# Two PSUM banks for the down products' halves, and five steps of VectorE and ScalarE moved up in a hybrid layer with sixteen experts

## The reference

```python
def reference(x, ...):                     # 1024 tokens x 1024, float32, one layer
    h = rms_norm(x, attn_norm_g)
    proj = h @ w_in                        # 1024 x 2824
    y_a = gated_delta_rule(...)            # 4 heads, chunks of 64, conv, gated norm
    y_b = swa_sink_attention(...)          # 8 query heads, 2 kv heads, window 128
    x = x + concatenate([y_a, y_b]) @ w_out
    return x + hier_moe(rms_norm(x, ffn_norm_g), ...)

def hier_moe(h, ...):                      # best of 4 groups, then best 2 of its 4 experts
    for e in range(16):
        gu = tok @ w_gate_up[e]            # 1024 -> 2 x 256
        act = silu(gu[:, :256]) * gu[:, 256:]
        y = y + gates[:, e:e + 1] * (act @ w_down[e])   # 256 -> 1024
    return y
```

## Time and profile before

| what | value |
|---|---|
| median of 3 runs | 946.41 us (943.29 to 948.25) |
| the profiled execution | 948.48 us, of which the span is 946.6 us |
| mean granted TensorE clock of it | 0.986 |
| TensorE busy | 889.7 us (94%) |
| VectorE busy | 603.7 us (64%) |
| ScalarE busy | 330.1 us (35%) |
| GpSimd busy | 222.6 us (24%) |
| HBM traffic | 137.7 MB, 145 GB/s over the span |

### The profile page before, as it was taken

The page is one execution under the profiler, slowest core; times in us unless marked ns, Lnnn a source line. Parts: engine busy times, 40 slices in busy tenths (PEclk is TensorE's granted clock), DMA queues, the critical chain, the costliest instruction groups (busy, mean ns, idle before and its releaser), DMA issues.

```text
span 946.6 us, 16441 instructions
## 1 busy us (share of the span) xinstructions
PE 889.7 (94%) x6148; PEld 591.6 (62%) x6148; DVE 603.7 (64%) x1746; ACT 330.1 (35%) x877; POOL 222.6 (24%) x302
## 2 busy tenths in 40 slices
PE   5999899999999999999999999789889999899986
PEld 5787587696696777768769656465533453433432
DVE  2367776785785787587678577868445535466443
ACT  1343331431432432332143134123363633646610
POOL 7020020020010001002002000300345546565643
PEclk9999999999999999999999999999989999999998
DMA  8920101010010120110100003703557968889621
GB/s 308 396 113 1 45 24 45 9 61 23 24 67 1 46 68 1 46 46 23 46 22 3 23 24 130 292 24 120 182 193 262 365 212 271 329 288 347 204 69 59
DMA packets 51052, 113.87 MB, mean 120 GB/s; under 512 B 11783, under 2 KB 13063, under 8 KB 50960
## 3 DMA queue, kind: packets, MB, share of 16 engines
q1 hardware_dynamic: 34064, 87.07, 25.8%
q0 software_dynamic: 14592, 25.22, 7.5%
q10 hardware_dynamic: 2304, 0.33, 0.2%
HBM read 112.56 MB, written 25.17 MB: 145 GB/s over the span
## 4 chain that ended last, share of the span: by engine, by line
PE 83%; DVE 10%; ACT 2%; issue 2%; DMA 1%; another core or an unknown queue 1%; POOL 0%; ACTq 0%; DVEq 0%; POOLq 0%
PE pm L432 77%; PE pm L435 5%; DVE pqkv L1519 2%; PE pm L836 1%; ACT ctmp L1247 1%; ACT pT L1247 1%; DMA qkvT<-h_mid,w_sb 0%; DMA xt<-in_x 0%; DVE xT L1342 0%; ACT pqkv L1038 0%; DVE xT L1455 0%; DVE X L1701 0%; DVE bs L1763 0%; DVE sc L1687 0%
## 5 line engine op out<-in xcount | busy, mean ns | idle before, releaser
L432 PEld LDWEIGHTS pm<-hT,w_sb 128*128 128x128 f32 x1544 | 176.6, 194 | 5.8 <-DVE hT L1471 3.0
L432 PE MATMUL pm<-hT,w_sb 128*128 128x128 f32 x1544 | 177.7, 277 | 2.3 <-DVE hT L1471 2.3
L432 PE MATMUL pm<-w_sb,hT 128*128 128x512 f32 (+1 forms) x384 | 153.8, 543 | 0.0
L432 PE MATMUL pm<-wo_sb,pT 128*128 128x512 f32 x320 | 143.9, 597 | 2.7 <-ACT pT L1110 1.4
L2071 POOL TENSOR_TENSOR tail<-tail,rows 128x512 f32<-128x512 f32 x8 | 10.8, 1344 | 483.9 <-ACT aTm L1059 483.9
L432 PEld LDWEIGHTS pm<-w_sb,hT 128*128 128x128 f32 x384 | 70.1, 193 | 51.8 <-issue 46.2
L432 PEld LDWEIGHTS pm<-wo_sb,pT 128*128 128x128 f32 x320 | 58.4, 190 | 68.0 <-issue 63.8
L1519 DVE SCALAR_TENSOR_TENSOR pqkv<-ci,cw,pqkv 128x128 f32<-128x128 f32 x288 | 77.4, 344 | 13.9 <-ACT pqkv L1038 13.8
L432 PE MATMUL pm<-w_sb,ctmp 128*128 128x512 f32 (+1 forms) x200 | 74.2, 601 | 0.6 <-DVE ctmp L1853 0.6
L432 PE MATMUL pm<-w_sb,Y 128*128 128x512 f32 x96 | 49.7, 637 | 8.4 <-issue 3.4
L1247 ACT ACTIVATE pT<-aTm 32x256 f32<-32x256 f32 x128 | 53.0, 414 | 9.6 <-DVE aTm L1930 8.1
(11 more groups left out here) (346 smaller groups left out, 1500.1 us busy)
## 6 DMA issues: line engine op xcount, KB each, us to landing
w_sb<-in_w_gate_up SPq DMA_DIRECT2D x12, 2048.0 KB
w_sb<-in_w_down SPq DMA_DIRECT2D x12, 1024.0 KB
wo_sb<-in_w_gate_up SPq DMA_DIRECT2D x4, 2048.0 KB
w_sb<-in_w_in SPq DMA_DIRECT2D x3, 2048.0 KB, 21.1
xt<-in_x SPq DMA_DIRECT2D x8, 512.0 KB, 4.6
xT<-in_x_turned SPq DMA_DIRECT2D x8, 512.0 KB, 3.8
w_sb<-in_w_in SPq DMA_DIRECT2D x4, 1024.0 KB, 13.0
wo_sb<-in_w_out SPq DMA_DIRECT2D x1, 4096.0 KB, 22.0
```

The lines of the kernel that those rows point to most:

```text
L432: return pe.matmul(o_, lhsT=l_, rhs=r_, start=start, stop=stop, skip_group_check=True)
```

## The change

1. `down_bank`: the left half of a whole tile's down product goes to pm[4], the right half to pm[5] (for all experts but the last, which has pm[1] and pm[0] as before). The right half waits for the right sum of the expert before (`added(i - 1, RIGHT)`), in step 1 for the second `table_ready`, since pm[5] held the sums of gates; the left half waits for the last sum of the expert before (`added(i - 1, FIRST)`). The first half tile's down product moves to pm[4] and waits for the left sum of its own expert.
2. ScalarE, step 0: the two `half_tanh` stand ahead of `spread_blocks(2)`.
3. VectorE, step 0: `turn_blocks(2)` stands ahead of the two copies of the table of gates.
4. VectorE, step 14: both `half_swiglu(14, c)` stand ahead of `add_out(13, 1)` and `add_half(13, 0)`.
5. VectorE, tile 0 and tile 6: `nn.gain_x` and `route_groups` stand at level 1.

```diff
         def down_bank(i, n):
 
-            return pm[1 - n] if i == NE - 1 else pm[4]
+            return pm[1 - n] if i == NE - 1 else pm[4 + n]
...
                     if i and i != NE - 1:
-                        pe.wait_ge(M.y_ready, added(i - 1, RIGHT))
+                        pe.wait_ge(M.y_ready, added(i - 1, FIRST if i < NE else RIGHT))
+                elif i == 0:
+                    pe.wait_ge(R.table_ready, 2)
                 elif i != NE - 1:
-                    pe.wait_ge(M.y_ready, added(i, LEFT))
+                    pe.wait_ge(M.y_ready, added(i - 1, RIGHT) if i < NE else added(i, LEFT))
...
-                bank = (pm[5], pm[2 + i % 2])[c]
+                bank = (pm[4], pm[2 + i % 2])[c]
...
-                if i and c == 0:
-                    pe.wait_ge(M.y_ready, added(i - 1, FIRST))
-                if i == 0 and c == 0:
-                    pe.wait_ge(R.table_ready, 1)
+                if c == 0:
+                    pe.wait_ge(M.y_ready, added(i, LEFT) if i < NE - 1 else added(i - 1, FIRST))
...
-                if i + 2 < NE:
+                if 0 < i < NE - 2:
                     spread_blocks(i + 2)
                 for c in range(2):
                     half_tanh(i, c)
+                if i == 0:
+                    spread_blocks(2)
...
-                    if l == 2 and nn and not pv:
+                    if l == 1 and nn and not pv:
                         nn.gain_x()
...
-                        if l == 2:
+                        if l == 1:
                             v.wait_ge(R.iotas, 1)
                             v.wait_ge(B.lg_ready, AHEAD)
                             route_groups(0, AHEAD)
...
                 if i == 0:
+                    turn_blocks(2)
                     v.wait_ge(R.gates_summed, 1)
...
-                    turn_blocks(2)
...
                 swiglu(i)
+                if i == NE - 2:
+                    half_swiglu(i, 0)
+                    half_swiglu(i, 1)
                 if i:
                     add_out(i - 1, 1)
                     add_half(i - 1, 0)
-                half_swiglu(i, 0)
-                half_swiglu(i, 1)
+                if i < NE - 2:
+                    half_swiglu(i, 0)
+                    half_swiglu(i, 1)
```

## The result

| | median us | from, to | executions |
|---|---|---|---|
| before | 946.35 | 943.29, 948.25 | 4 |
| changed | 934.06 | 931.97, 936.0 | 4 |

A forecast was written before the change was run, and what follows sets the result against it. TensorE, busy 889.7 of 946.6 us, was taken as the bound. Terms 5.2 + 6.5 + 1.7 + 1.2 + 1.8 = 16.4 take the profiled 948.5 to 932.1, a median of 930.0; range 926 to 937.

The forecast's parts named there:

- Two banks: Down products in seven expert steps: right half no longer waits for the left sum; 5.2 us, bounds 2.8 to 6.0.
- The 0.35 of issue: Issue gap read ahead of 735.00; if it stayed at every right half, the banks would give only 2.8 us.
- The new waits: Left product for the previous expert's half-tile sum, half product behind left in pm[4]; both forecast to cost nothing, except in step 14.
- First half tiles: Step 1: stall of 3.93 goes, 3.2 of clock returns, new wait costs 0.6; 6.5 us, bounds 4.5 to 7.2.
- The cover of 1.0: Step 1: inputs for expert 1's half products ready at 697.2, TensorE there at 698.2, so no new stall.
- Last half tiles: Step 14: half gating ahead of expert 13's sums lets the left product start earlier; 1.7 us, bounds 1.0 to 1.9.
- The tiles: Attention tiles 0 and 6: VectorE work moved one level up shortens TensorE's stalls; 1.2 and 1.8 us.
- a base load or a GpSimd transfer of the kind feared: Rival, experts: GpSimd's loads come later than VectorE's sums need them, costing about 5 us: 935; chance 0.07.
- the branches: Rival, experts: two skipped branches ahead of the right half cost 0.35, first term only 2.8: 932.5; chance 0.05.
- The moves do nothing: Rival: the wait that mattered was another, so the time stays 946.4; chance 0.02.
- No clock fell for alternating banks: Rival, expert steps: alternating banks with short gaps drops TensorE's clock, 1.8 more per column half, 957; chance 0.02 (slower).
- The remote wait of VectorE: VectorE once waited 4.75 for something called remote, costing TensorE 1.2; such events may recur anywhere, included in the range.

The follow-up runs named there:

- The run with the stalls filled: Kernel before plus unneeded products ahead of the stalled level-4 product, two calls in tile 0, one in tile 6: 944.23 against 947.2 us, ratio 0.9975.
- the first measurement: Changed kernel against the kernel before: median 934.06 against 946.35 us, ratio 0.9873.
- the second measurement: Changed kernel unaltered, measured again beside the experiments, against the kernel before: median 927.71 us, ratio 0.981.
- the third measurement: Changed kernel unaltered, measured once more beside the experiments, against the kernel before: median 927.69 us, ratio 0.9803.
- the first filling at `l == 4`: Kernel before plus unneeded products ahead of the level-4 product, five calls in tile 0 and three in tile 6: ratio 1.0003.

## Why the prediction was right, and what it missed

The forecast was 930.0, the measurements 934.06, 927.71 and 927.69, all inside 926 to 937.

- **Two banks**: forecast 5.2. Right in mechanism and size: 5.4 in the traces, 5.4 alone, and 4.2 when taken out of the changed kernel. The 0.35 of issue that set the lower bound never came between left and right. The new waits (left for the half tile's sum, half product for left) show in no row of TensorE. The row of the wait decided. The Trainium skill (TensorE: Matmul & The Clock Gate, section "HAM oscillation — how this bites in real kernels") tells of a kernel in which double buffering of PSUM gave no further gain. By it this term would have been near 0, and the runs here show 5.4.
- **First half tiles**: forecast 6.5, measured 5.9 net in the profiled execution and 6.0 [4.4 to 7.6] alone. The stall went, the clock came back with it, and the new wait was 0.57 to 0.64 for a forecast of 0.6. The cover of 1.0 for expert 1's half products held: in none of the three profiled executions of the changed kernel did they wait for VectorE. The 0.9 that the first profiled execution lost within and behind them has another cause, and nothing in the working stands for it.
- **Last half tiles**: forecast 1.7, 1.7 in both profiled executions that tell it apart, 3.3 by the times. Mis-sized by about 1.0, if the reading above holds: the 2.03 of idleness was priced by an execution in which the clock did not fall behind it, and in four of the other six it did.
- **The tiles**: forecast 1.2 and 1.8, and the stalls shrank by 1.24 and 1.87. But the term was mis-sized: it held half of what the two moves gave, 6.1 alone. The working took the stall's length and did not look at the clock behind it, though it did exactly that for step 1. The twelve products stood in the same timeline with 7.11; a window behind each stall would have shown 0.50. In the profiled execution this is 3.4 us missing from the sum of 16.4; over executions, with the lower level behind three stalls of four, 2.6. The run with the stalls filled shows it. With it the sum is 19.0, against the 18.0 and 18.7 measured. That the forecast median lies between the first measurement and the later ones is in part luck: this term was too small by 2.6, and losses such as the 4.3 of the first profiled execution, which the sum has no term for, go the other way.
- **The first measurement** came out at 12.3 and not at 18. In its profiled execution step 4, step 8 and the 0.9 of step 1 can be named, 4.3 us (the late start can't: the profiled execution of the second measurement has 1.90 of idleness at the same place). Why all four of its executions were above ten of the eleven later ones is open. Chance in so few is unlikely, and the clock isn't it: two had a mean clock of 0.991 and took 936, two had 0.994 and 0.995 and took 932, while executions of the second measurement at 0.994 took 926.65 and 929.35. The kernel before gave 946.4 in the first measurement and 946.6 and 947.2 in the later ones, so a slower chip isn't it either.
- **The rivals**: TensorE's waits have no row for a base load or a GpSimd transfer of the kind feared, and the branches stayed hidden. VectorE does wait for such loads (2.35 for the base in hT in the third measurement), without a wait of TensorE behind it. "The moves do nothing" is refuted by each part alone. No clock fell for alternating banks: in the three traces of the changed kernel the lower level stands in the experts only behind idle times of 1.26 and 2.05 and at the program's end, where the kernel before has it too. The Trainium skill (the same page, section "A second HAM failure mode: psum-queue depth-cycling") tells of a kernel that cycles through banks and whose clock oscillates. No run here shows that. The remote wait of VectorE was named as a risk and did come: twice at the place where it was before, with 1.10 and 2.05 of idleness on TensorE, and once behind a sum of step 12, with 1.26.

## What to carry to other kernels

For every stall of TensorE read the granted clock and the duration of the products behind it, and compare these with the same products elsewhere; a stall of 1.8 or 2.6 us cost another 1.7 here in three executions of four, one of 2.0 in about half, and one of 3.9 another 3.2. Since this varies from execution to execution, one trace prices a stall too high or too low: look at several. A stall that can't be removed may still be filled with products that aren't needed, but with fewer than the stall holds: measure one first. And when work is moved ahead of a copy that someone waits for, look whether a part of it can stay in front.

## What the runs showed of the hardware

The fall of the clock is not fixed by the place or the length of the idle time: 2.57, 2.03 and 1.79 were followed by the lower level in some traces and not in others, and so executions of one kernel can differ by steps of about 1.7 us. Single stalls of 1.10, 1.21 and 1.32 in these traces were followed by no such stretch, nor were 0.85 and 0.94, but the 1.26 behind VectorE's late sum of step 12 was. In the routing, where stalls of 0.8 to 1.1 follow each other within a few us, the traces show between one and two such stretches, of 1.7 or 3.4 lost each: 609 to 613 in the first trace of the changed kernel (1.7), 605 to 612 and 618 to 626 in the third (3.4 each).

VectorE's wait before ci in step 8, 3.9 to 4.8 us, occurs in the kernel before, in the one with only the last half tiles' gating, and in two of three traces of the changed kernel. Such waits also stand before single sums (in the changed kernel 5.43 before one in tail at 890.06, when TensorE's product had ended at 888.18), and so they do in the kernel before with the first filling at `l == 4` (5.30), so they aren't the change's alone. The trace gives no semaphore for them, no run here was aimed at them, and their cause stays open.
